# A delta-rule mixer reworked: units of four heads in a pipeline over two buffer sets, the keys' norm by a power on GpSimd

## What is computed

```python
kk = (k * k_k).reshape(bsz, seq, H, N)
kk = kk / jnp.maximum(jnp.sqrt(jnp.sum(kk * kk, axis=-1, keepdims=True)), 1e-12)
k = k * (1.0 + (a - 1.0) * k_a)
...
def step(state, inp):
    r_t, w_t, k_t, v_t, a_t, b_t = inp          # a_t = -kk, b_t = kk * a
    sa = jnp.einsum('bhij,bhj->bhi', state, a_t)
    state = (state * w_t[:, :, None, :] + sa[..., None] * b_t[:, :, None, :]
             + v_t[..., None] * k_t[:, :, None, :])
    return state, jnp.einsum('bhij,bhj->bhi', state, r_t)
...
y = ((y - mean) * lax.rsqrt(var + RWKV_LNX_EPS)).reshape(bsz, seq, D_MODEL)
y = y * lnx_g + lnx_b
bonus = jnp.sum(r_h * k_h * r_k, axis=-1, keepdims=True) * v_h
y = y + bonus.reshape(bsz, seq, D_MODEL)
return (y * g) @ w_o
```

## Time and profile before

| | us |
|---|---|
| median of three runs | 3959.67 |
| the profiled execution | 3963.83 |
| its span | 3962.0 |
| TensorE busy in it | 3571.5 |
| VectorE busy | 1844.4 |
| ScalarE busy | 1377.7 |
| GpSimd busy | 145.0 |
| the mixer of layer 3 | from 1400 to about 1881 |

### The profile page before, as it was taken

The page is one execution under the profiler, slowest core; times in us unless marked ns, Lnnn a source line. Parts: engine busy times, 40 slices in busy tenths (PEclk is TensorE's granted clock), DMA queues, the critical chain, the costliest instruction groups (busy, mean ns, idle before and its releaser), DMA issues.

```text
span 3962.0 us, 47260 instructions
## 1 busy us (share of the span) xinstructions
PE 3571.5 (90%) x20284; PEld 2926.0 (74%) x20284; DVE 1844.4 (47%) x2906; ACT 1377.7 (35%) x2365; POOL 145.0 (4%) x181
## 2 busy tenths in 40 slices
PE   7988989998999988588998998997998999799898
PEld 6976979864988965376797986984564887656697
DVE  4524555533555435642455524542334555603476
ACT  3423444422444422010444423431441434302354
POOL 0000000011000000110000000000002000000100
PEclk9997999998999988676999997998998999899999
DMA  6541545456544432622554542532002332422252
GB/s 226 183 132 65 181 155 191 143 169 204 191 165 160 150 113 85 213 75 70 186 183 152 193 123 75 182 107 63 18 25 96 106 127 109 137 85 75 86 184 103
DMA packets 421534, 523.45 MB, mean 132 GB/s; under 512 B 53927, under 2 KB 363804, under 8 KB 421196
## 3 DMA queue, kind: packets, MB, share of 16 engines
q1 hardware_dynamic: 420524, 518.33, 39.8%
q0 software_dynamic: 800, 2.10, 0.2%
HBM read 518.29 MB, written 2.10 MB: 131 GB/s over the span
## 4 chain that ended last, share of the span: by engine, by line
PE 84%; DVE 8%; ACT 3%; POOL 2%; DMA 1%; issue 1%; SPq 0%; POOLq 0%; DVEq 0%; ACTq 0%
PE ps L176 17%; PE ps L184 17%; PE ps L185 17%; PE ps L186 17%; PE ps L194 3%; PE ps L958 3%; PE ps L272 2%; PE ps L1134 1%; PE ps L1561 1%; PE ps L411 1%; POOL small L464 1%; PE ps L2637 1%; POOL junk L2373 1%; ACT junk L505 1%; DVE a L1953 1%
## 5 line engine op out<-in xcount | busy, mean ns | idle before, releaser
L184 PE MATMUL ps<-a 128*128 128x256 f32 (+1 forms) x4488 | 1426.8, 318 | 53.8 <-DVE a L554 35.0
L185 PE MATMUL ps<-a 128*128 128x256 f32 (+1 forms) x4488 | 1424.1, 317 | 0.0
L186 PE MATMUL ps<-a 128*128 128x256 f32 (+1 forms) x4488 | 1420.8, 317 | 0.0
L184 PEld LDWEIGHTS ps<-a 128*128 128x128 f32 x4488 | 866.9, 193 | 117.0 <-issue 22.1
L186 PEld LDWEIGHTS ps<-a 128*128 128x128 f32 x4488 | 865.7, 193 | 54.2
L185 PEld LDWEIGHTS ps<-a 128*128 128x128 f32 x4488 | 866.9, 193 | 51.7
L685 DVE TENSOR_TENSOR a<-ring,a 128x1024 fp32r<-128x1024 f32 x594 | 693.5, 1221 | 371.4 <-ACT a L679 371.4
L679 ACT ACTIVATE a<-ring 128x1024 fp32r<-128x1024 f32 x594 | 585.8, 1048 | 280.8 <-PE ps L186 226.4
L176 PE MATMUL ps<-ring,xt 128*128 128x512 f32 (+1 forms) x640 | 263.5, 571 | 6.4 <-ACT xt L1068 2.9
L776 ACT ACTIVATE tmp<-ps 128x256 f32<-128x256 f32 x176 | 67.4, 383 | 520.0 <-PE ps L186 520.0
L176 PEld LDWEIGHTS ps<-ring,xt 128*128 128x128 f32 x640 | 118.9, 192 | 144.3 <-issue 135.2
(11 more groups left out here) (325 smaller groups left out, 3243.6 us busy)
## 6 DMA issues: line engine op xcount, KB each, us to landing
ring<-in_ffn_w_in_dram SPq DMA_DIRECT2D x220, 1024.0 KB, 7.2
ring<-in_ffn_w_out_dram SPq DMA_DIRECT2D x121, 1024.0 KB, 5.0
...
```

What stands on the lines that cost most here:

```text
L184: pe.x.matmul(out, lh, rh, start=start and i == 0, stop=False)
L185: pe.x.matmul(out, lh, rl, start=False, stop=False)
L186: ins = pe.x.matmul(out, ll, rh, start=False, stop=stop and i == n - 1)
```

## The change

1. The modulation is made in pairs: 16 products into one bank, one ACT copy of 512 columns, four transposes, one DVE sum.
2. The keys' norm: GpSimd raises the maximum to the power -0.5, one instruction of 128x256 for each k, in place of the ACT square root and the DVE reciprocals. The two products behind it run two steps later in the same DVE loop.
3. Order on TensorE: k, then half of r between the sums of squares, the other half of r between the decays; the gate and the value projection move behind the small products `cg`, then the bonus, then 14 modulation columns, then the units. Transposed carried tiles come one k later.
4. k and b lie side by side and are multiplied by one instruction. The products with r (the receptance) move to GpSimd, three products over whole tiles, as does the bonus' product.
5. The blocks for t = 1 are copied by ACT, those for t = 0 by DVE, without a mask. No modulation stands inside the recursion.
6. Units: eight units (t, g) of four heads with two sets of buffers. In step i unit i = v begins (products, first doubling, z), unit i-1 = u ends (second doubling, u, y, s1) and unit i-2 = w is normed. Each step has two modulation columns. The level masks are made by DVE from PSUM; GpSimd builds the block-diagonal tiles of each unit by two products with a mask.
7. The norm, gate and bonus are per unit: three DVE products over 256 columns; gain, shift and gate are multiplied beforehand by GpSimd over 1024 columns.

The core of the diff ("..." marks what is left out; the loads of k and r also move ahead of the gate's):

```diff
+def pe_ada_products(K, pe, rot):
+    s3, s, m0 = v3(K.sc32, 32), K.s, pe.ada
+    bank, freed = rot.take(s.act, "ada row", m0)
...
+    for n in range(2):
+        c = K.w["ada", m0 + n]
+        wv = v3(c.buf, 256)
+        pe.wait_ge(*c.landed)
+        for k in (0, 2, 4, 6, 1, 3, 5, 7):
+            g = k // 2 * 32
+            ins = pe.x.matmul(bank[g:g + 32, n * 256:n * 256 + 256], s3[:, k, :], wv[:, k, :], start=k % 2 == 0, stop=k % 2 == 1)
+        ins.then_inc(*s.pe.up("ada", m0 + n))
...
+def pe_ada_turns(K, pe, rot):
+    s, m0 = K.s, pe.ada
+    pe.ada += 2
+    bank, freed = rot.take(s.dve, "ada sum", m0)
...
+    pe.wait_ge(*s.act.at("ada row", m0))
+    flips(K, pe, bank, [K.adarow[:, tk(n)] for n in range(4)]).then_inc(*s.pe.up("ada flip", m0))
...
-        act.x.activation(K.adarow[m % 2], K.place["ada row", m][:, 0:256], AF.Copy).then_inc(*s.act.up("ada row", m))
+        act.x.activation(K.adarow, K.place["ada row", m], AF.Copy).then_inc(*s.act.up("ada row", m))
...
-    load_row(K, sp, (tag, "lg"), I["rwkv_lnx_g"][0], D, (s.dve, (tag, "y gain", 1)))
-    load_row(K, sp, (tag, "lb"), I["rwkv_lnx_b"][0], D, (s.dve, (tag, "y bias", 1)))
-    sp_ada(K, sp, 14)
...
+    load_row(K, sp, (tag, "lg"), I["rwkv_lnx_g"][0], D, (s.pool, (tag, "gain", 1)))
+    load_row(K, sp, (tag, "lb"), I["rwkv_lnx_b"][0], D, (s.pool, (tag, "shift", 1)))
+    sp_ada(K, sp, RWKV_ADA + 18)
...
-    pe.wait_ge(*s.dve.at(tag, "mix", 0))
-    pe_projA(K, pe, (tag, "r"), D, M.M0, T, rot, s.act)
     for k in range(8):
+        if k % 2 == 0:
+            pe_rwkv_r(K, pe, M, k // 2, rot)
         bank, freed = rot.take(s.dve, tag, "kk sum", k)
         pe.wait_ge(*s.act.at(tag, "kk sq", k))
         pe.wait_ge(*freed)
         pe.x.matmul(bank[:, 0:T], K.c("blk"), M.BT[:, k, :], start=True, stop=True).then_inc(*s.pe.up(tag, "kk sum", k))
...
+        if k % 2:
+            pe_rwkv_r(K, pe, M, 4 + k // 2, rot)
+        if k:
+            pe_rwkv_carried(K, pe, M, rot, k - 1)
+    pe_rwkv_carried(K, pe, M, rot, 7)
+    pe.wait_ge(*s.dve.at(tag, "hat", 7, 1))
...
+            pe_rwkv_heads(K, pe, M, banks, 0, t, g, M.BT, KK).then_inc(*s.pe.up(tag, "cg", t, g))
+    g2 = K.w[tag, "g2"]
...
+    pe.wait_ge(*s.dve.at(tag, "mix", 3))
+    pe_projB(K, pe, (tag, "v"), D, M.MV, (0, 1), rot, lambda i: s.act)
+    bank, freed = rot.take(s.dve, tag, "bonus")
+    pe.wait_ge(*freed)
+    pe.wait_ge(*s.pool.at(tag, "rk"))
...
+    ins.then_inc(*s.pe.up(tag, "bonus"))
+    pe_ada(K, pe, RWKV_ADA, rot)
+    rot = Turns(K, range(4, 8))
+    for i in range(9):
+        pe_rwkv_step(K, pe, M, rot, i, RT, KK)
     pe_ada(K, pe, 2, rot)
...
+def pe_rwkv_step(K, pe, M, rot, i, RT, KK):
...
+        bank, freed = rot.take(s.act, tag, u, "x", 6)
+        pe.wait_ge(*freed)
+        pe.wait_ge(*s.dve.at(tag, u, "l6"))
+        pe.wait_ge(*s.dve.at(tag, u, "tn"))
+        for n in range(4):
+            ins = pe.x.matmul(bank[:, tk(n)], P.L6[:, n, :], P.TN[:, n, :], start=True, stop=True)
+        ins.then_inc(*s.pe.up(tag, u, "x", 6))
...
+    if v is not None:
+        banks = pe_rwkv_pair(K, pe, M, i, 0, "l6")
+        pe_rwkv_heads(K, pe, M, banks, 0, t, g, M.BT, KK)
+        pe_rwkv_heads(K, pe, M, banks, 256, t, g, M.KT, KK).then_inc(*s.pe.up(tag, v, "ak"))
+    if u is not None:
+        bank, freed = rot.take(s.dve, tag, u, "tt", 6)
+        pe.wait_ge(*freed)
+        pe.wait_ge(*s.act.at(tag, u, "x", 6))
+        pe.wait_ge(*s.dve.at(tag, u, "tt", 5))
+        for n in range(4):
+            ins = pe.x.matmul(bank[:, tk(n)], P.XB[:, n, :], P.TT[:, n, :], start=True, stop=True)
+        ins.then_inc(*s.pe.up(tag, u, "tt", 6))
...
+        banks = pe_rwkv_pair(K, pe, M, i, 2, "rk")
+        pe_rwkv_heads(K, pe, M, banks, 0, t, g, M.BT, RT)
+        pe_rwkv_heads(K, pe, M, banks, 256, t, g, M.KT, RT).then_inc(*s.pe.up(tag, v, "rb"))
+        pe_ada_products(K, pe, rot)
+        bank, freed = rot.take(s.act, tag, v, "x", 5)
+        pe.wait_ge(*freed)
+        pe.wait_ge(*s.dve.at(tag, v, "l5"))
+        pe.wait_ge(*s.pool.at(tag, v, "tn"))
+        for n in range(4):
+            ins = pe.x.matmul(bank[:, tk(n)], S.L5[:, n, :], S.TN[:, n, :], start=True, stop=True)
+        ins.then_inc(*s.pe.up(tag, v, "x", 5))
+        bank, freed = rot.take(s.act, tag, v, "z")
+        pe.wait_ge(*freed)
...
+        pe.wait_ge(*s.dve.at(tag, v, "ak"))
+        if t:
+            pe.wait_ge(*s.dve.at(tag, v - 4, "s1"))
...
+                ins = pe.x.matmul(bank[:, o * 64:(o + 1) * 64], S.AK[:, o, :], vs[:, h * 64:(h + 1) * 64], start=t == 0, stop=t == 0 or m == 1)
+        ins.then_inc(*s.pe.up(tag, v, "z"))
+    if u is not None:
+        bank, freed = rot.take(s.act, tag, u, "u")
+        pe.wait_ge(*freed)
+        pe.wait_ge(*s.act.at(tag, u, "z"))
+        pe.wait_ge(*s.dve.at(tag, u, "tt", 6))
...
+    if v is not None:
+        bank, freed = rot.take(s.dve, tag, v, "tn")
+        pe.wait_ge(*freed)
+        pe.wait_ge(*s.act.at(tag, v, "x", 5))
+        for n in range(4):
+            ins = pe.x.matmul(bank[:, tk(n)], S.TT[:, n, :], S.XB[:, n, :], start=True, stop=True)
...
+        bank, freed = rot.take(s.dve, tag, u, "centred")
+        pe.wait_ge(*freed)
+        pe.wait_ge(*s.dve.at(tag, u, "rk"))
+        pe.wait_ge(*s.act.at(tag, u, "u"))
...
+        ins.then_inc(*s.pe.up(tag, u, "y"))
+        if tu == 0:
+            bank, freed = rot.take(s.dve, tag, u, "s1")
...
+    if v is not None:
+        pe_ada_turns(K, pe, rot)
...
+            if i >= 4:
+                act.wait_ge(*s.dve.at(tag, "hat", (i - 4) // 2, t))
...
+            act.wait_ge(*s.dve.at(tag, "bt", k))
+            act.x.activation(M.EB[:, k, tk(t)], b[:, 0:128], AF.Exp, scale=-EXPM).then_inc(*s.act.up(tag, "decay", k, t))
+        if k % 2:
+            act_rwkv_r(K, act, M, 4 + k // 2, RT)
+        if k:
+            act_rwkv_carried(K, act, M, k - 1)
+    act_rwkv_carried(K, act, M, 7)
...
+        act.wait_ge(*s.pe.at(tag, v, "x", 5))
+        act.x.activation(M.sets[v % 2].XB, v3(K.place[tag, v, "x", 5], 128), AF.Copy).then_inc(*s.act.up(tag, v, "x", 5))
+        act.wait_ge(*s.pe.at(tag, v, "z"))
+        act.x.activation(M.sets[v % 2].Z, K.place[tag, v, "z"][:, 0:256], AF.Copy).then_inc(*s.act.up(tag, v, "z"))
+    if u is not None:
+        act.wait_ge(*s.pe.at(tag, u, "u"))
+        act.x.activation(M.sets[u % 2].U, K.place[tag, u, "u"][:, 0:256], AF.Copy).then_inc(*s.act.up(tag, u, "u"))
...
+    for i in range(10):
+        if i < 8:
+            dve.wait_ge(*s.pe.at(tag, "kk sum", i))
+            dve.x.tensor_scalar(BT[:, i, :], K.place[tag, "kk sum", i][:, 0:T], 1e-24, None, MAXOP).then_inc(*s.dve.up(tag, "kk sum", i))
+        if i >= 2:
+            k = i - 2
+            dve.wait_ge(*s.pool.at(tag, "kk norm", k))
+            dve.x.tensor_tensor(KK[:, k, :], KK[:, k, :], BT[:, k, :], MULT).then_inc(*s.dve.up())
+            dve.wait_ge(*s.dve.now())
+            dve.x.scalar_tensor_tensor(out=BT[:, k, :], in0=KK[:, k, :], scalar=-1.0, in1=AT[:, k, :], op0=MULT, op1=MULT).then_inc(
+                *s.dve.up(tag, "bt", k))
...
-        rn = BT[:, k, :]
-        dve.x.reciprocal(rn, rn).then_inc(*s.dve.up())
...
+                dve.x.tensor_tensor(v3(cb, 128), KB[:, k, :, p], bc(e[:, 256:384], 1, [128, 2, 128]), MULT).then_inc(*s.dve.up(tag, "carry", k))
+            dve.x.tensor_tensor(KB[:, k, :, p], KB[:, k, :, p], bc(e[:, 0:128], 1, [128, 2, 128]), MULT).then_inc(*s.dve.up())
             dve.x.tensor_tensor(KK[:, k, p], KK[:, k, p], e[:, 128:256], MULT).then_inc(*s.dve.up(tag, "hat", k, t))
...
+    dve.wait_ge(*s.pe.at(tag, "bonus"))
+    dve.x.tensor_copy(M.bonus, K.place[tag, "bonus"][:, 0:32]).then_inc(*s.dve.up(tag, "bonus"))
+    dve_ada(K, dve, RWKV_ADA)
+    for i in range(10):
+        dve_rwkv_step(K, dve, M, i)
+        if i == 8:
+            dve_ada(K, dve, 2)
...
+        dve_rwkv_mask(K, dve, M, v, S.L5, 0, 0, lev[:, 5 * 128:6 * 128], "l5")
+    if u is not None:
+        P = M.sets[u % 2]
+        dve.wait_ge(*s.pe.at(tag, u, "tt", 6))
+        dve.x.tensor_tensor(P.TT, P.TT, v3(K.place[tag, u, "tt", 6], 128), ADD).then_inc(*s.dve.up(tag, u, "tt", 6))
+    if v is not None:
+        dve_rwkv_mask(K, dve, M, v, S.AK, 0, 256, strict, "ak")
...
+        dve.wait_ge(*s.act.at(tag, w, "sq"))
+        dve.x.tensor_reduce(ss, v3(M.sq, 64), AX.X, ADD).then_inc(*s.dve.up(tag, w, "ss"))
+        dve_mean(K, dve, (tag, w), rs, ss, 64, 64e-5, 1.0)
+    if v is not None:
+        dve_rwkv_mask(K, dve, M, v, S.L6, 0, 0, lev[:, 6 * 128:7 * 128], "l6")
+        dve.wait_ge(*s.pe.at(tag, v, "rb"))
+        dve_rwkv_mask(K, dve, M, v, S.RB, 2, 0, incl, "rb")
+        dve_rwkv_mask(K, dve, M, v, S.RK, 2, 256, incl, "rk")
+        if v == 0:
+            dve.wait_ge(K.s_b, 16 * 8)
+            dve.x.transpose(M.ttc, M.tnc).then_inc(*s.dve.up(tag, "ttc"))
...
+        dve.wait_ge(*s.pool.at((tag, w), "rs"))
```

(49 more changed lines are left out.)

730 lines of the change are left out of this document (311 added, 419 removed).

## The result

The changed kernel takes 4169.8 us (median, 4164.3 to 4173.4) where the kernel before takes 3959.7: a ratio of 1.053 with an interval of 1.051 to 1.055. It is 5.3% slower. The forecast was 4177 us.

A forecast was written before the change was run, and what follows sets the result against it. Eight GpSimd powers, 327 us unhidden, were to bound the edited stage; its output projection moves from 1878.4 to 2093, +214.6. 3963.8 + 214.6 + 3.5 = 4182, median 4 lower; 4177 us forecast, range 4100 to 4240.

The forecast's parts named there:

- The power's price: Keys' norm: one GpSimd power of 256 columns costs 40.9 us by a straight line, eight 327 us.
- Rival A: Keys' norm: a power costs like GpSimd's product, 0.64 us; 3870 us total; not slower under about 13 us each; chance 0.07.
- rival B: Keys' norm: a long row is cheaper than the line, 20 to 33 us a power, 4010 to 4115; chance 0.08.
- Nothing hides it: Keys' norm: all engines' queues stand behind the eight powers from 1462.3 to 1789.3, so nothing covers their 327 us.
- Decays: Loop over k behind the powers, from 1791 to the heads' products at 1823: 32 us, bounds 24 and 42.
- Gate: Gate's product on TensorE, now beside the recursion: 8.5 us.
- The small tiles and the recursion: Behind the heads' products: copies 11 us, DMA round 14.3 us, recursion 39.5 us, ending at 1888.
- The units' start: Behind the 14 modulation columns on TensorE: 1911, held by the modulation's weights and no longer by the small DMAs.
- A unit: Each packed unit of four heads takes 21 us; 16.5 at the high clock, 32 at the low one.
- GpSimd's hole: In the units, GpSimd's power and two products hold TensorE up to 2 us at high clock, none at low.
- Rival C: Units don't pack, wait on hand-overs at a low clock: 27 us a unit, 42 us more, 4219; chance 0.10.
- The pairing in the other mixer: Gated linear attention: two modulation columns share one ScalarE copy, costing +3.5 us, bounds 0 and 5.

The follow-up runs named there:

- experiment 3: Changed kernel with GpSimd's power over only the first 128 or 32 columns of each tile, the others by root and reciprocal: 4010.1 us and 3884.2 us.
- Experiment 2: Kernel before the change, with only square root and reciprocal replaced by the eight GpSimd powers: 4255.3 us, ratio 1.075.
- the first experiment: Changed kernel with only the power undone, ScalarE's square root and VectorE's reciprocal back: 3865.8 us, ratio 0.977.
- Experiment 5: Changed kernel with root and reciprocal back, plus gate and value projection moved ahead of the heads' products: 3889.0 us.
- experiment 6: Changed kernel with root, reciprocal and GpSimd's unit blocks ahead of the norm's power, plus receptance products ahead of small DMAs: 3845.6 us.
- experiment 7: Root, reciprocal, blocks ahead of norm's power; 10 modulation columns before units, not 14: 3842.4 us; 8, with early receptance products: 3842.2 and 3841.5.
- Experiment 4: Changed kernel with root and reciprocal back, plus GpSimd's blocks first, ahead of an older unit's norm power: 3843.4 us, ratio 0.971; later 3846.6.

## Why the prediction was right

**The power's price, right.** The whole forecast hung on one number, 40.9 us for an instruction of which the trace before had only 1, 4 and 16 columns. It took 41.13, and experiment 3 shows the straight line at 32 and 128 columns too. Rival A (the power costs like a product) and rival B (a bend in the line) fall with it. Rival A's break-even, 13 us a power, comes out at 15 by experiment 3.

**Nothing hides it, right.** Powers from 1463.8 to 1792.6 were forecast from 1462.3 to 1789.3. Experiment 2 put them in the old order, where they cost 294 us: no order of the two hides them, as every queue ends up behind the keys.

**What is left without the power, right.** Rival A's sum for a kernel whose power is cheap, 3870 us, can be held against the first experiment, which has none: 3865.8. The terms behind the power are the same as in the main sum, with the same errors.

**Decays, 32 us forecast, 24 measured.** The clock was 0.90 in that stretch right behind 329 us of near idleness; I had bounds of 24 and 42 and took too careful a middle.

**Gate, 8.5 us forecast, 16.09 measured.** The term was taken from a row at the high clock. Its new place is behind the small tiles' products, a stretch of short products with gaps (5.30 us busy of the 10.1 from 1817.4 to 1827.5), and TensorE's granted clock was 0.50 while the gate's products ran. Experiment 5 shows both prices of the same 16 products, 16.09 and 8.39.

**The small tiles and the recursion, right at their end by luck.** From the last copy to the recursion's first row the forecast had 14.3 us; it took 8.4 (1829.5 to 1837.9). The 14.3 came from a place where modulation weights ran beside the small DMAs (DMA share 0.88; GpSimd stood 4.78 us for its stores), and now none did (share 0.37, 1.93 us). The recursion was put at 39.5 and took 49, by GpSimd's products beside it (experiment 6). With the decays, 6 us sooner, the errors cancel: it ended at 1887, forecast 1888. I had costed the receptance on GpSimd at nothing, on the ground that TensorE wants it late: that looked at who waits for the result, not at whom the instruction holds while it runs.

**The units' start, 1911 forecast, 1922 measured.** The cause named, modulation weights and not the small tile, was right: TensorE was busy 22.6 of 34 us from 1888 to 1922 at a DMA share of 1.07, and experiment 7 moves the start by 12.7 us. Little of the 11 us is the gate's: it took 7.6 us more but began 6.8 sooner (1827.5, forecast 1834.3), and the value projection, 3 us longer, ended at 1874, forecast 1870. The rest is the weights: TensorE waited for those of the 14th column until 1918.4, forecast 1909.

**A unit, 21 us forecast, 18.6 measured.** The clock was mis-sized: 0.75 to 0.82 was taken from the chunks, 0.89 was granted from 1939 to 2080. With 0.89 the prediction's own formula gives 18.5 us. That it then fits is partly luck, as two of its terms failed in opposite ways. The floor at the high clock was put at 16.5 and is 13.8. Of this, 1.7 us come from 32 records that have 64 rows, of which 16 take 1.09 us, not 1.95; another 0.5 from the count, 116 square records and not 120. The chain of the kernel with blocks first shows a whole step without a hole:

```profile
1634.92 1.13 PE ps L1707 x8
1636.05 1.09 PE ps L1554 x16
1637.14 1.09 PE ps L1721 x8
1638.23 1.09 PE ps L1554 x16
1639.32 1.86 PE ps L409 x32
1641.18 1.09 PE ps L1733 x8
1642.27 0.84 PE ps L1747 x8
1643.11 0.89 PE ps L1755 x8
1644.01 0.95 PE ps L1762 x8
1644.95 0.89 PE ps L1767 x8
1645.85 2.68 PE ps L176 x24
```

The other term is GpSimd's hole. I gave it up to 2 us and none at the low clock; it was 2.8 in steps 2 to 6, each time behind products at the high clock, so that its size at the low clock stays open. Experiment 4 shows that it cost the high clock in some steps too. Rival C (27 us a unit, they don't pack) is excluded by 18.6.

**The pairing in the other mixer,** put at +3.5: the edited mixer starts 1.2 us later than before. This says little, as in experiment 2, which has no pairs, it starts 3.9 us later than before. The term was not tried alone and is not shown.

At the output projection the errors are +11.2 us for the units' start, -1.1 for step 0, -16.7 for the seven units and -1.0 for the end: together -7.6 on 214.6. That the two large ones cancel in part is luck; what made the forecast right is the power's 327 us. The prediction's range has a slip that changes nothing: its parts add to -63 us and not to -65.
